# Hybrid attention and expert block on one core: the next unit's projections in NSA units, cut into pieces of half the length in both halves of each step

## The reference

```python
proj = rms_norm(x, ln1) @ w_in          # 2048 -> 5688 columns
o_a = diff_attention(...)               # 4 heads: softmax - lam * softmax, t5 bias
o_b = forgetting_attention(...)         # 8 heads, cumulated log-forget-gates
o_c = nsa_attention(...)                # 16 heads in 4 groups: compressed, selected and window keys, gated
x = x + concat(o_a, o_b, o_c) @ w_out
x = x + hier_moe(rms_norm(x, ln2), ...) # top 2 of 64 experts per token
return rms_norm(x, ln_f)
```

## Time and profile before

| | |
|---|---|
| median of 3 runs | 2085.79 us (2085.25 to 2086.55) |
| profiled execution | 2086.53 us, span of the core 2084.0 us |
| TensorE | busy 1812.9 us (87%), mean granted clock 0.950 |
| VectorE | busy 612.2 us (29%) |
| ScalarE | busy 472.1 us (23%) |
| POOL | busy 430.2 us (21%) |
| DMA | 527 MB, mean 253 GB/s |

### The profile page before, as it was taken

One profiled execution on the slowest core, in us unless ns is written; L12 is line 12 of the kernel. 1 busy time (PEld: TensorE's weight loads), 2 busy tenths in 40 slices (PEclk: granted clock), 3 DMA queues, 4 the chain that ended last, 5 costly groups with the idle time before them and its releaser, 6 DMA issues.

```text
span 2084.0 us, 28021 instructions
## 1 busy us (share of the span) xinstructions
PE 1812.9 (87%) x11148; PEld 1284.7 (62%) x11148; DVE 612.2 (29%) x1432; ACT 472.1 (23%) x992; POOL 430.2 (21%) x478
## 2 busy tenths in 40 slices
PE   6999999999999999999788878888878888888880
PEld 4877777777777767788745445555455555455540
DVE  4321223544766667410421111111111111111115
ACT  5222233332534444322211100110100101101101
POOL 2422333341000023444011111111111111111100
PEclk9999999999999999999789999999999999999995
DMA  9453233233321231151679999999999999999976
GB/s 279 116 141 88 77 81 81 61 82 71 61 52 41 72 122 41 62 170 64 252 310 423 426 427 425 425 426 425 426 427 424 424 426 424 425 423 423 420 333 245
DMA packets 190056, 527.22 MB, mean 253 GB/s; under 512 B 65650, under 2 KB 148850, under 8 KB 162074
## 3 DMA queue, kind: packets, MB, share of 16 engines
q1 hardware_dynamic: 171498, 509.18, 63.6%
q0 software_dynamic: 18480, 16.97, 2.4%
HBM read 530.38 MB, written 46.02 MB: 277 GB/s over the span
## 4 chain that ended last, share of the span: by engine, by line
DMA 33%; PE 14%; DVE 1%; SPq 1%; issue 1%; ACT 0%; DVEq 0%; POOLq 0%
DMA ht_region<-in_w_up 32%; PE PJ L1160 11%; PE PJ L1161 2%; PE S L1180 1%; SPq L698 1%; DMA ht_region<-y_scratch 1%; DVE ring_region L1904 0%; DVE mix_region L1895 0%; DVE mix_region L1894 0%; PE PT L1143 0%; DMA y_scratch<-ring_region,s_idx 0%; DMA x_region<-h_scratch,g_idx 0%; DVE ring_region L1846 0%; SPq L729 0%; DVEq L310 0%
## 5 line engine op out<-in xcount | busy, mean ns | idle before, releaser
L875 PE MATMUL PJ<-ht_rounded,ring_rounded 128*128 128x512 f32 (+1 forms) x928 | 321.2, 400 | 4.9 <-ACT at_region L1277 4.9
L1160 PE MATMUL PJ<-at_region,ring_region 128*64 128x256 f32 x1024 | 254.9, 412 | 63.3 <-DMA at_region<-in_w_up 62.4
L1160 PE MATMUL PJ<-ht_region,ring_region 128*64 128x256 f32 x1024 | 244.9, 401 | 50.6 <-DMA ht_region<-in_w_up 50.6
L1161 PE MATMUL PJ<-at_region,ring_region 128*64 128x256 f32 x1024 | 255.6, 413 | 0.0
L1161 PE MATMUL PJ<-ht_region,ring_region 128*64 128x256 f32 x1024 | 245.7, 402 | 0.0
L1160 PEld LDWEIGHTS PJ<-at_region,ring_region 128*64 128x64 f32 x1024 | 150.1, 149 | 148.3 <-issue 91.0
L1160 PEld LDWEIGHTS PJ<-ht_region,ring_region 128*64 128x64 f32 x1024 | 145.8, 145 | 131.4 <-issue 77.5
L804 POOL DMA_INDIRECT y_scratch<-ring_region,s_idx x64 | 64.7, 1012 | 781.3 <-DVE ring_region L1860 766.9
L752 POOL TENSOR_TENSOR ring_rounded<-ring_region,ring_rounded 128x512 fp32r<-128x512 f32 x100 | 127.2, 1303 | 464.3 <-ACT ring_rounded L1222 464.3
L875 PEld LDWEIGHTS PJ<-ht_rounded,ring_rounded 128*128 128x128 f32 (+1 forms) x928 | 173.2, 190 | 55.3 <-issue 14.4
L1852 DVE TENSOR_TENSOR ring_region<-ring_region,PJ 64x256 f32<-64x256 f32 x64 | 27.1, 423 | 595.5 <-ACT ring_region L1437 595.5
(11 more groups left out here) (273 smaller groups left out, 2735.3 us busy)
## 6 DMA issues: line engine op xcount, KB each, us to landing
at_region<-in_w_gate SPq DMA_DIRECT2D x32, 2048.0 KB
at_region<-in_w_down SPq DMA_DIRECT2D x32, 2048.0 KB
at_region<-in_w_up SPq DMA_DIRECT2D x32, 2048.0 KB
ht_region<-in_w_gate SPq DMA_DIRECT2D x32, 2048.0 KB
ht_region<-in_w_up SPq DMA_DIRECT2D x32, 2048.0 KB
x_region<-in_w_down SPq DMA_DIRECT2D x32, 2048.0 KB
ring_region<-in_w_in SPq DMA_DIRECT2D x36, 1024.0 KB, 5.9
ring_region<-in_w_out SPq DMA_DIRECT2D x16, 1024.0 KB, 5.1
```

What stands on the lines that cost most here:

```text
L875: ins = mm(out, w[:, k, 0:width], h[:, k, :], start=k == 0 and i == 0, stop=k == KT - 1 and i == 2)
L1160: mm(GU[0:CAP, 0:D_EXPERT], x, gate[:, j, :], start=j == 0, stop=j == KT - 1)
L1161: ins = mm(GU[CAP:2 * CAP, 0:D_EXPERT], x, up[:, j, :], start=j == 0, stop=j == KT - 1)
```

## The change

`fillings()` gives nsa units both halves of each step as slots, as diff and fox units have them.

```diff
     for g in range(len(HEADS) - 1):
         lo, hi = max(START[g] - LOOK, 0), START[g + 1] - LOOK
-        slots = [(n, half) for n in range(lo, hi) for half in range(2 if len(STEPS[HEADS[g][0]]) == NT else 1)]
+        slots = [(n, half) for n in range(lo, hi) for half in range(2)]
```

## The result

| | before | after |
|---|---|---|
| median | 2075.35 us (20 runs, 2072.21 to 2086.55) | 2086.95 us (20 runs, 2079.55 to 2089.11) |
| ratio | | 1.0044, 95% interval 1.0031 to 1.0057 |
| profiled execution | 2086.53 us, span 2084.0 | 2085.72 us, span 2083.2 |

The ratio is +9.1 us on 2075.35 (6.4 to 11.8); the medians themselves lie 11.6 us apart. I had forecast +5.6, slower, and 2091.4 us. One thing has to be known to read the numbers: the runs of the kernel before lie in two groups, 12 of the 20 at 2072 to 2076 and 8 at 2085 to 2087. The three runs and the profiled execution from which the prediction worked were all of the upper, rarer group. So the two profiled executions have almost the same time, and the comparison has to be made where the change acts, not at the end.

What follows compares the result with a forecast made beforehand. The prediction took TensorE's issue and waits to bound the NSA units. Its terms, -11.5 + 11.7 + 2.7 + 2.7 = +5.6 us, on a median of 2085.79 gave 2091.4 us, range 2085.3 to 2096.5.

Steps and rivals of the forecast that it cites:

- Turn: Steps 32, 48, 64: TensorE waits 2.3 us for ScalarE's copy of turned v; with clock falls 11.7 us added.
- k tile: Steps 44, 60, 76: waits for VectorE's scaling and their low clock go, -11.5 us; later copies stall, +2.7.
- its own list of signs: Profile signs against the prediction: turn waits absent or under 1 us, clock staying 1.00, new waits at 6-matmul pieces.
- Short pieces: NSA units: 16 more pieces each cost 0.9 us per unit, 2.7 us in all.
- the clock term of the sum: NSA waits: a 1.6 us fall behind each of three removed and three added waits, 0 behind step 76's.
- five of five fell: Attention stages: the clock fell after all five waits of this size, three of 2.24 us and two of 2.9.
- The second rival: New turn waits come without a clock fall after each: 2086.6 us with none, 2089.8 with two; chance 0.31.
- The third rival: Falls of 6.8 us, or one after step 76's 1.9 us wait: 1.7 us more each, 2093 to 2097; chance 0.13.
- the clock of those 10 us is worth nothing either way: From step 77's transposes to step 80's first output product: a ScalarE and POOL chain sets the time, 0 us.
- The faster rival: ScalarE reaches the turned tile's copy in time, no turn stall: -6.1 us, 2079.7 us; chance 0.08.

Runs made afterwards that it cites:

- split_only: The kernel before with its NSA pieces cut in two, one per half, turn and k tile's end unmoved: 2076.96 us, ratio 1.0007.
- turn_half0: The changed kernel with v in six pieces instead of seven, so its turn is back in half 0 of the next step: 2073.49 us, ratio 0.9988 to before.
- before_again: The kernel before, unchanged, run again for a second trace: 2076.01 us, ratio 1.0012.
- turn_half1: The kernel before with whole pieces, only v's turn moved to half 1 of the step where v ends: 2087.60 us, ratio 1.0072.
- after_again: The changed kernel, unchanged, run again for a second trace: 2086.50 us, ratio 1.0048 to before.
- k_last_late: k_last with ScalarE's rounding behind the exponentials and VectorE's k tile copy behind the scaling, from step 32 on: 2077.35 us, ratio 1.0006 to before.
- turned_first: The changed kernel with ScalarE's copy of the turned tile ahead of the exponentials in steps 32, 48, 64: 2076.66 us, ratio 1.0006 to before.
- k_last: The kernel before with the sixteenth slot used too, whole pieces, k tile ending in half 0 of steps 44, 60, 76: 2068.68 us, ratio 0.9963.
- k_last_76: k_last with ScalarE's rounding behind the exponentials and VectorE's k tile copy behind the scaling, in step 76 only: 2066.82 us, ratio 0.9953 to before.
- k_last_76_25: k_last_76 with ScalarE's rounding also put behind the copy of the turned tile in step 25: 2062.96 us, ratio 0.9940 to before.

## Why the prediction was right in the waits and wrong in the price

**Right, by its own steps.** The direction; the place and mechanism of each wait; the sizes. Turn: 2.3 said, 2.41 measured, three times. k tile: three waits of 2.24 gone; 0.4, 0.4 and 1.9 said, 0.28, 0.29 and 1.87 measured. The idle time of the stretch rose by 4.0 us; 6.9 + 2.7 - 6.7 = 2.9 was forecast, and the rest is 3 x 0.1 at the turns, less 0.3 at the k tile, plus 1.0 of small waits in steps 29 to 32 and at the short pieces (0.34 at 507.89 and 0.43 at 513.21 are the largest; by its own list of signs such new waits spoke against it). Short pieces: 2.7 said, +1.7 in the rest (1.1 in split_only, 2.9 in turn_half0, against before).

**The step that failed: the clock term of the sum.** I put one fall of 1.6 us behind each wait, three taken away and three added, so that it cancelled, and none behind step 76's wait. Over all traces that contain them:

| wait | followed by a fall | lost on average |
|---|---|---|
| 2.24 us (steps 44, 60, 76; before, before_again, turn_half1, split_only) | 8 of 12 | 1.1 us |
| 2.41 us (steps 32, 48, 64; after, after_again, turn_half1) | 8 of 9, three of them 6.8 us long | 2.1 us |
| 2.32 us (steps 45, 61; k_last_late) | 2 of 2 | 1.7 us |
| 1.87 us (step 76; after, after_again, turned_first, k_last, turn_half0) | 3 of 5 | 1.0 us |
| 1.50 us (step 78; k_last_late, k_last_76, k_last_76_25) | 2 of 3 | 1.1 us |
| 1.0 to 1.4 us (turned_first, k_last_late, k_last_76_25) | 0 of 6 | 0 |
| 2.54 us (at 148 to 152 us; all twelve) | 5 of 12 | 0.7 us |
| 2.92 us (at 166 to 169 us; all twelve) | 12 of 12, five of them 6.8 us long | 2.4 us |
| 2.94 us (step 25; all but k_last_76_25) | 11 of 11, two of them 6.8 us long | 2.0 us |

The averages are half of 3.4 or 6.8 us by these counts, an estimate. The counts are small, and length alone does not order them: the waits of 2.92 and 2.94 us were always followed by a fall, but 2.54 us less often than 2.24 and 1.87. The term is then -3 x 1.1 + 3 x 2.1 + 1.0 = +4.0 us where I had 0. Directly, in the two traces of each kernel, the low clock in the stretch costs 6.5 us after and 4.2 before, +2.3, and the fall that reaches past its end some 0.6 more. With the +4.0, the measured idle time (+4.0) and the pieces (+1.7) the change comes to +9.7; the stretches give +8.0, (270.1 + 271.4 - 263.5 - 262.0) / 2, and +0.6 behind it.

The ratio says +9.1, but that agreement is in part luck. The ratio takes in both groups of the kernel before, and the traces that I have of them, one of each, differ mostly by time lost outside the stretch. The trace of the lower group, before_again, and the two of the changed kernel differ by 11.1 us in span: 8.7 in the stretch, 0.6 behind it, and 0.8 ahead of step 29 and 1.0 behind the start of step 80, where the change does nothing.

In the prediction's words, what failed is "five of five fell", read as a rule and as one size. The gain was priced by the one execution in which all three old waits had lost the clock. The second rival, equal waits with unequal ends, was right as a mechanism, but I turned it only upon the new waits, as a hope for a smaller loss. It held for the old ones too, and there it takes from the gain. The third rival, with a chance of 0.13, came closest for the new waits: step 48 had a fall of 6.8 us and step 76's wait had one too, in both traces of the changed kernel.

**Wrong: the base.** The forecast was +5.6 on the upper group, given as 2091.4. The execution that I worked from was 11.6 us longer than the second trace of the same kernel, and the median of 20 runs is 2075.35, not 2085.79. The time after, 2086.95, fell into my range by luck: the base was 10.4 us too high and the price too low.

**Wrong in part: "the clock of those 10 us is worth nothing either way".** In the two traces of the changed kernel the fall behind step 76's wait reaches past step 77's transposes, and the way to step 80 is 11.2 in place of 10.5 to 10.6 us.

**The faster rival** (turn stall stays out, -6.1) gives the right sign by the stretch for the kernel in which it is kept out, but not its size: turn_half0 is -2.5 us by the ratio, with an interval from -6.2 to +1.2. The stretch is 3.1 to 4.6 us shorter than before. The missing part is the short pieces and small waits. With whole pieces and the turn where it was, k_last has it.

**Open.** Why the runs of the kernel before lie in two groups so far apart was seen in one trace of each group only, and that the upper group's other runs lost their time in the same place is not shown. Why the 2.41 us of step 48 had the long fall each time, and the equal waits of steps 32 and 64 a short one or none, is not settled either. Nor is it shown that the new waits lose the clock more often than the old ones by anything but their places in these few traces.

## What to carry to other kernels

A wait is removed by moving a step, and the step takes its queue along: before moving a copy to another slot, list what stands ahead of it in its engine's order at the new place, and compare that with what the waiting engine still has to do. Here one slot more or less for one tile was worth 13 us, and the gain at the k tile could be had from one line, without the rest. And price a wait that may cost the clock by several executions, on the side that goes as well as on the side that comes.

## What the runs showed of the hardware

The clock fell after much shorter waits than the 2.24 us that the prediction started from: after 1.87 us in 3 of 5 cases and after 1.50 in 2 of 3, but after 1.0 to 1.4 us in none of 6. Length alone did not decide: the 2.54 us at 148 to 152 us, the same in all twelve traces, was followed by a fall in five, and the 2.92 and 2.94 us in the fox steps in all 23 cases, seven of them 6.8 us long. Three of the nine waits of 2.41 us were followed by 6.8 us at the low clock, five by 3.4, one by none, though the waits are equal to 0.02 us. And taking 1.40 us from a wait of 2.41, in three places, was worth some 10 us by the medians. In the stretch 4.2 of them are the waits themselves, and 4.5 and 5.9 (against the two traces of the changed kernel) are the falls that no longer came.
